# Two chained transformer stacks in one kernel: the residual scaled and rounded piece by piece from its PSUM bank, with some turns, loads and waits moved

## What is computed

```python
def rms_norm(x, g):
    y = x * lax.rsqrt(jnp.mean(x * x, axis=-1, keepdims=True) + RMS_EPS)
    return y * g
def swiglu(x, w13, w2):
    gate, up = jnp.split(x @ w13, 2, axis=-1)
    return (jax.nn.silu(gate) * up) @ w2
# for each layer i of each block, with its gains g[0..7]:
h = h + 0.5 * rms_norm(swiglu(rms_norm(h, g[0]), ffn_w13[i, 0], ffn_w2[i, 0]), g[1])
h = h + rms_norm(mixer(rms_norm(h, g[2])), g[3])
h = h + 0.5 * rms_norm(swiglu(rms_norm(h, g[4]), ffn_w13[i, 1], ffn_w2[i, 1]), g[5])
gate = jax.nn.sigmoid(rms_norm(h, g[6]) @ ple_w_gate[i])
h = h + rms_norm(gate * (p[i] @ ple_w_proj[i]), g[7])
```

## Time and profile before

| | us |
|---|---|
| median of three executions | 2274.13 |
| the profiled execution, its own time | 2272.61 |
| its span, first to last instruction | 2270.8 |
| TensorE busy | 2236.9 (99%) |
| VectorE busy | 1467.1 (65%) |
| ScalarE busy | 1154.9 (51%) |
| GpSimd busy | 180.8 (8%) |

### The profile page before, as it was taken

How to read it: one execution, slowest core, us unless ns; L and a number is a source line. 1 busy time by engine, 2 the same in 40 slices (tenths; PEclk the granted TensorE clock), 3 DMA queues, 4 the chain that set the end, 5 groups by cost and what they waited for, 6 DMA issues and landing times.

```text
span 2270.8 us, 33812 instructions
## 1 busy us (share of the span) xinstructions
PE 2236.9 (99%) x13395; PEld 1820.5 (80%) x13395; DVE 1467.1 (65%) x2079; ACT 1154.9 (51%) x1668; POOL 180.8 (8%) x286
## 2 busy tenths in 40 slices
PE   8999999999999999999999999999999999999998
PEld 6888888888888758878887888878888788868887
DVE  6656757656765877576567656656656765677655
ACT  5445545445544454254455445455445544565444
POOL 1001001001000010420011001001001100051001
PEclk9999999999999999999999999999999999999999
DMA  7556655554655640065556555524555555526553
GB/s 260 183 190 204 230 171 192 186 184 167 213 185 187 203 158 12 8 221 184 185 175 200 185 186 194 189 96 156 184 188 190 187 185 185 194 78 199 185 177 111
DMA packets 290091, 395.61 MB, mean 174 GB/s; under 512 B 11752, under 2 KB 193328, under 8 KB 289936
## 3 DMA queue, kind: packets, MB, share of 16 engines
q1 hardware_dynamic: 285072, 377.20, 50.3%
q0 software_dynamic: 4720, 16.20, 2.1%
q10 hardware_dynamic: 144, 0.07, 0.0%
HBM read 392.37 MB, written 1.05 MB: 173 GB/s over the span
## 4 chain that ended last, share of the span: by engine, by line
PE 94%; DVE 3%; ACT 1%; issue 1%; POOL 0%; DMA 0%; DVEq 0%; POOLq 0%; SPq 0%; ACTq 0%
PE bank L516 28%; PE bank L518 27%; PE bank L517 27%; PE bank L542 2%; PE bank L530 1%; PE bank L2560 0%; PE bank L2554 0%; ACT wh L637 0%; PE bank L1451 0%; ACT JUNK L644 0%; PE bank L2571 0%; PE bank L1966 0%; PE bank L1188 0%; DVE H L890 0%; PE bank L2531 0%
## 5 line engine op out<-in xcount | busy, mean ns | idle before, releaser
L823 DVE TENSOR_TENSOR wl<-raw,wh 128x1024 fp32r<-128x1024 f32 x708 | 859.0, 1223 | 554.8 <-ACT wh L637 554.4
L637 ACT ACTIVATE wh<-raw 128x1024 fp32r<-128x1024 f32 x708 | 744.2, 1058 | 648.1 <-PE bank L518 622.5
L516 PE MATMUL bank<-wh,XH 128*128 128x512 f32 x2000 | 801.0, 400 | 5.2 <-DVE wl L823 2.9
L518 PE MATMUL bank<-wh,XL 128*128 128x512 f32 x2000 | 780.7, 390 | 0.0
L517 PE MATMUL bank<-wl,XH 128*128 128x512 f32 x2000 | 780.5, 390 | 0.0
L516 PEld LDWEIGHTS bank<-wh,XH 128*128 128x128 f32 x2000 | 375.9, 188 | 94.5 <-issue 17.1
L518 PEld LDWEIGHTS bank<-wh,XL 128*128 128x128 f32 x2000 | 375.9, 188 | 81.6
L517 PEld LDWEIGHTS bank<-wl,XH 128*128 128x128 f32 x2000 | 376.5, 188 | 72.1 <-issue 0.5
L516 PE MATMUL bank<-wh,AH 128*128 128x512 f32 x704 | 276.0, 392 | 0.0
L518 PE MATMUL bank<-wh,AL 128*128 128x512 f32 x704 | 274.2, 389 | 0.0
L517 PE MATMUL bank<-wl,AH 128*128 128x512 f32 x704 | 274.1, 389 | 0.0
(11 more groups left out here) (339 smaller groups left out, 1725.3 us busy)
## 6 DMA issues: line engine op xcount, KB each, us to landing
raw<-in_ffn_w_dram SPq DMA_DIRECT2D x182, 512.0 KB, 4.7
raw<-in_ffn_wi_dram SPq DMA_DIRECT2D x176, 512.0 KB, 4.7
raw<-in_ffn_w_dram SPq DMA_DIRECT2D x40, 1024.0 KB, 4.9
raw<-in_ffn_wo_dram SPq DMA_DIRECT2D x40, 1024.0 KB, 4.8
raw<-in_a_wqkv_dram SPq DMA_DIRECT2D x18, 1024.0 KB, 4.8
raw<-in_a_w_in_dram SPq DMA_DIRECT2D x16, 1024.0 KB, 5.2
raw<-in_b_w_in_dram SPq DMA_DIRECT2D x12, 1024.0 KB, 4.9
bc<-in_norm_g_dram POOLq DMA_DIRECT2D x16, 512.0 KB, 5.2
```

Source lines behind the costliest of these rows:

```text
L516: pe.e.matmul(o, a, h, start=(k == 0), stop=False)
L518: m = pe.e.matmul(o, b, h, start=False, stop=(k == layer.nk - 1))
L637: act.e.activation(self.wh[j % N_W][:, 0:p.size], self.raw[p.chunk % N_RAW][:, p.at:p.at + p.size], ACT.Copy).then_inc(*self.rounded.up(j))
L823: dve.e.tensor_tensor(self.wl[j % N_W][:, 0:p.size], self.raw[p.chunk % N_RAW][:, p.at:p.at + p.size], self.wh[j % N_W][:, 0:p.size].bitca ...
```

## The change

- CT and the counter x_scaled are gone. ScalarE now writes XH in four instructions of 128 x 128 for each half, straight from the bank, with the gain as scale. VectorE writes XL in four `scalar_tensor_tensor` of 128 x 128: bank by gain, minus XH. They begin when all four of the half's XH are there. TensorE waits for single squares instead of halves. The bank is free after the last XL of its half.
- Tile 1's turns: steps 8 and 9 in a stage that follows ple or dilated, steps 6 and 7 in all others, stage 0 included.
- Stage 0: tile 1 of x is loaded behind chunk 1; its scaling stands ahead of part 4 instead of part 2; the six `pe_keep` matmuls at step 4 are gone.
- `dve_out`: at the last part of the first half, the result is weighed before that part's `leave`.
- RWKV: LoRA steps 18, 22, 26, 30; ScalarE's `act_mixed(2, 1, 1)` behind th; `pe_keep` in (0, 1) and (1, 1) instead of (0, 1) and (1, 0).

```diff
     def x_ready(self, n):
-        return lambda k, t: [(self.x_hi, n, t, k // 4), (self.x_lo, n, t, k // 4)]
+        return lambda k, t: [(self.x_hi, n, t, k), (self.x_lo, n, t, k)]
     def pe_turn_own(self, pe, n, step):
-        first = 6 if n else 2
+        first = 6 if n == 0 else 8 if STAGES[n - 1][0] in ("ple", "dilated") else 6
     def pe_turn_x(self, pe, n, t, b):
-        bank = self.turn_bank(pe, ("x", n, t, b), (self.x_scaled, n, t, b))
+        bank = self.turn_bank(pe, ("x", n, t, b), (self.x_lo, n, t, 4 * b + 3))
...
         def up(step):
-            if n == 0 and step == 4:
-                pe.wait_all(self.bank_busy[1])
-                self.pe_keep(pe, self.bank(1), 6)
...
+    def x_parts(self, n, t, k):
+        block, c = self.gains(n)
+        turned = self.bank(self.place["turn", ("x", n, t, k // 4)])[:, (k % 4) * P:(k % 4 + 1) * P]
+        to = [x[:, k, t * P:(t + 1) * P] for x in (self.XH, self.XL)]
+        if STAGES[n][0] == "dilated":
+            turned = turned.rearrange("p (b c) -> p c b", c=4)
+            to = [x.rearrange("p (c b) -> p c b", c=4) for x in to]
+        return turned, self.GT[:, block, c + k:c + k + 1], *to
     def act_x_hi(self, act, n, t, b):
-        act.wait_ge(self.x_scaled, n, t, b)
-        act.e.activation(self.XH[:, 4 * b:4 * b + 4, t * P:(t + 1) * P], self.CT[b][:, :, :], ACT.Copy).then_inc(
-            *self.x_hi.up(n, t, b))
+        act.wait_ge(self.consts, "gains" if self.gains(n)[0] == 0 else "gains2")
+        act.wait_ge(self.turned, "x", n, t, b)
+        for k in range(4 * b, 4 * b + 4):
+            turned, gain, hi, _ = self.x_parts(n, t, k)
+            act.e.activation(hi, turned, ACT.Copy, scale=gain).then_inc(*self.x_hi.up(n, t, k))
...
-    def dve_x_lo(self, dve, n, t, b):
-        hi, lo = (x[:, 4 * b:4 * b + 4, t * P:(t + 1) * P] for x in (self.XH, self.XL))
-        dve.wait_ge(self.x_hi, n, t, b)
-        dve.e.tensor_tensor(lo, self.CT[b][:, :, :], hi.bitcast(F32), ALU.subtract).then_inc(*self.x_lo.up(n, t, b))
+    def dve_x_lo(self, dve, n, t, b):
+        dve.wait_ge(self.consts, "gains" if self.gains(n)[0] == 0 else "gains2")
         dve.wait_ge(self.turned, "x", n, t, b)
+        dve.wait_ge(self.x_hi, n, t, 4 * b + 3)
+        for k in range(4 * b, 4 * b + 4):
+            turned, gain, hi, lo = self.x_parts(n, t, k)
+            dve.e.scalar_tensor_tensor(lo, turned, gain, hi.bitcast(F32), ALU.mult, ALU.subtract).then_inc(
+                *self.x_lo.up(n, t, k))
     def dve_x(self, dve, n, t):
-        for b in range(2):
-            self.dve_x_scale(dve, n, t, b)
         for b in range(2):
             self.dve_x_lo(dve, n, t, b)
...
             if i == half - 1:
-                self.leave(dve, p.j + N_W)
                 for t in range(T):
                     self.dve_weigh(dve, n, 0, t, self.pair((n, "out", 0))[t])
+                self.leave(dve, p.j + N_W)
...
             self.load(sp, c)
-            if c == 0:
+            if c == 1:
                 tokens(1)
...
-        if step in (17, 21, 25, 29):
-            b, t = divmod((step - 17) // 4, 2)
+        if step in (18, 22, 26, 30):
+            b, t = divmod((step - 18) // 4, 2)
...
-            self.act_mixed(act, 2, *divmod(i, 2))
+            if i < 3:
+                self.act_mixed(act, 2, *divmod(i, 2))
         if i == 3:
...
+            self.act_mixed(act, 2, 1, 1)
...
-        if (t, o) in ((0, 1), (1, 0)):
+        if o == 1:
             self.pe_keep(pe, banks[0], 6 - t)
```

More of the change, by code:

```diff
@@ L311, in __init__ @@
         self.AL = at("AL", EO + FF // P * S * 4, [P, FF // P, S], F32R)
-        self.CT = [at(f"CT{i}", EO + 54784 + 2048 * i, [P, 4, P], F32) for i in range(2)]
         self.gU = at("gU", EO + 32768, [P, T, 2048], F32)
@@ L417, in __init__ @@
         self.used = [count(f"used{t}") for t in range(T)]
-        self.turned, self.x_scaled, self.x_hi, self.x_lo = (
-            count(x) for x in ("turned", "x_scaled", "x_hi", "x_lo"))
+        self.turned, self.x_hi, self.x_lo = (count(x) for x in ("turned", "x_hi", "x_lo"))
         self.squared, self.rs = count("squared"), count("rs")
@@ L722, in act_start @@
                 self.act_x_hi(act, 0, 0, j)
-            if j == 2:
+            if j == 4:
                 for b in range(2):
@@ L824, in leave @@
                             self.wh[j % N_W][:, 0:p.size].bitcast(F32), ALU.subtract).then_inc(*self.left.up(j))
[L826 to L830, removed]
-        dve.wait_ge(self.turned, "x", n, t, b)
[L832 to L841, removed]
-    def dve_x_lo(self, dve, n, t, b):
-        hi, lo = (x[:, 4 * b:4 * b + 4, t * P:(t + 1) * P] for x in (self.XH, self.XL))
-        dve.wait_ge(self.x_hi, n, t, b)
-        dve.e.tensor_tensor(lo, self.CT[b][:, :, :], hi.bitcast(F32), ALU.subtract).then_inc(*self.x_lo.up(n, t, b))
+    def dve_x_lo(self, dve, n, t, b):
+        dve.wait_ge(self.consts, "gains" if self.gains(n)[0] == 0 else "gains2")
+        dve.wait_ge(self.turned, "x", n, t, b)
+        dve.wait_ge(self.x_hi, n, t, 4 * b + 3)
[3 more added lines that the diff above has]
+                *self.x_lo.up(n, t, k))
     def dve_x(self, dve, n, t):
-        for b in range(2):
-            self.dve_x_scale(dve, n, t, b)
         for b in range(2):
@@ L926, in dve_start @@
         dve.e.memset(self.NEG[:, :], -0.5).then_inc(*self.neg.up())
-        for b in range(2):
-            self.dve_x_scale(dve, 0, 0, b)
         self.dve_x_lo(dve, 0, 0, 0)
@@ L932, in dve_start @@
         self.leave(dve, 1)
-        self.dve_x(dve, 0, 1)
         for j in range(2, N_W):
+            if j == 4:
+                self.dve_x(dve, 0, 1)
             self.leave(dve, j)
```

## The result

Eleven executions of the changed kernel have a median of 2281.54 us (2278.71 to 2291.44), eleven of the kernel before 2274.13 us. The ratio is 1.0031 with a 95% interval of 1.0020 to 1.0041: slower by 0.3%. The profiled execution took 2278.71 us, its span is 2276.9: 6.1 us more than the one before.

What follows compares the result with a forecast made beforehand. TensorE, busy 99% of the span, was taken to bound the kernel. Terms 3.45 + 2.9 - 1.4 - 0.75 - 1.1 - 1.2 - 0.2 gave +1.7: 2274.3 us profiled, 2275.8 median; range 2270.0 to 2282.0.

Steps and rivals of the forecast that it cites:

- the entries to ple: Four boundaries into ple stages: lose nothing, as part 3 is there three steps into the second layer.
- the clock: Rival: TensorE's clock falls in the new stalls; one fall gives 2277.5, two 2279.2, four 2282.6 us; chance 0.33.
- The pieces: Four 128 x 128 instructions per half: ScalarE's end after 1.15 us, VectorE's after 1.14; next may start at 1.06.
- Cheaper: Rival: ScalarE's and VectorE's four hold no more than one copy and one subtraction, 2270.1 or 2267 us; chance 0.17.
- Dearer: Rival: strided dilated reads or VectorE's bank reads cost 0.1 us more a piece, +5 to +8; chance 0.15.
- ple to ffn: Stages 4, 8, 12: VectorE's chain 0.75 us late plus 0.4 for the later turn, together +3.45 us.
- The small boundaries: Stages 1, 2, 9, 13, 14: 0.55 us lost in four places, up to 0.75 at stage 1, together +2.9.
- dilated: Dilated to ffn: with the turn at step 8 the residual is there, -1.4 us.
- rwkv: Rwkv to ffn: weighing in VectorE's idle time makes the residual 1.1 us earlier; -0.75 us net.
- LoRA: RWKV's LoRA step: th no longer behind act_mixed and the product a step later, -1.1 us.
- scan: RWKV scan: extra matmuls of (1, 0) cover nothing and go, those in (1, 1) fit an idle; -1.2 us.
- The start: Stage 0: step 9 at 20.1 against 20.36 us, -0.2, after an idle of 2.2.

Runs made afterwards that it cites:

- the pieces undone: The changed kernel with scale, rounding and rest of x done by whole halves through CT again: 2272.02 us, ratio 0.9986 to the kernel before.
- the turn put back: The changed kernel with tile 1's turns back at steps 6 and 7 behind ple stages: 2281.41 us, ratio 1.0025 to the kernel before.
- the pieces alone: The kernel before with only the four-instruction x_hi and x_lo straight from the bank added: 2284.64 us, ratio 1.0044 to the kernel before.

## Why the prediction came out right

2281.54 lies in the range, 2270 to 2282, but only half a microsecond below its upper end, and outside the forecast's own range, 2273.5 to 2278. The wide range held because it was drawn around the rivals too; that the time fell just inside it is partly luck. Slower by over 0.2% had a chance of 0.32, same 0.58, and it came out slower by 0.3%. The forecast was +1.7 us, the medians are 7.4 apart. From 2275.8 to 2281.5 it is two steps: 1.2 us at the entries to ple, and the clock. The other terms missed by at most 0.3 each, and these misses cancel.

**The pieces** were sized right: four hold ScalarE for 1.02 and end after 1.14 (1.06 and 1.15 forecast), VectorE's four take 1.13 (1.14). An instruction on a bank with a scale and one on tiles in SBUF were good rows for the new ones. ("Those rows read SBUF" is wrong for rows 3: their source is a bank.) "Cheaper" fell: four pieces hold ScalarE for 1.02 and VectorE for 1.04, not for 0.53 and 0.61. The Trainium skill (VectorE: DVE Perf Modes, The TRN2 errata) has the cycles from which the prediction estimated 0.25 us for a piece. A single piece is 375 ns long by the groups, but in a row of four they follow each other after 0.26, so the estimate fits the spacing and not the length. It never led to a chain on time and a sum of -3.7, as the prediction has it: four times 0.25 hold ScalarE for 1.0, nearly the forecast's own 1.06. "Dearer" fell too: the dilated boundary gave 1.55. The Trainium skill (PSUM — Partial Sum Buffer, PSUM bank collisions raise a hardware error) has two engines in one bank as an error even where both read; that fits x_lo waiting for the fourth XH of its half, which was not varied here.

**ple to ffn** held to 0.1 a place. Its two terms stand apart in the runs: 0.7 goes with the pieces undone (0.75 forecast), 0.5 with the turn put back (0.4). That part 3 ends the stall is shown by moving it: the stall at step 7 goes, and 1.75 of its 2.7 comes off the time.

**The small boundaries** were sized 0.3 too high in sum, most of it at stage 1, which lost 0.45 where the prediction took no slack and 0.75.

**The entries to ple** are the step that failed: "lose nothing, part 3 is there three steps into the second layer, and that cover is over 2 us". That is right for the weight part; the turn at step 6 was not priced. Before, it had 0.5 us of slack behind the residual, and the chain was 0.8 late:

```profile
536.98 1.41 DVE L890 SCALAR_TENSOR_TENSOR H<-TMP,ST,H 128x512 f32<-128x512 f32 x2
...
538.34 0.60 PE L530 MATMUL bank<-ident,H 128*128 128x128 f32 x4
```

```profile
540.33 1.41 DVE L881 SCALAR_TENSOR_TENSOR H<-TMP,ST,H 128x512 f32<-128x512 f32 x2
541.23 0.63 PE L527 MATMUL bank<-ident,H 128*128 128x128 f32 x4 [0.15 <-DVE H L881]
```

The idle reads 0.15, the loss is 0.3 (541.23 less 538.34 is 2.89, where the steps before were 2.56 late): TensorE's rows are 0.39 long but 0.23 apart, so a wait is read from start to start.

**The gains** (dilated, rwkv, LoRA, scan) held within 0.15 each. The run with these alone has all four, and loses 0.9 elsewhere.

**The start** was right for step 9 (20.41, forecast 20.1, idle 2.29 for 2.2) and so for its own term; the fall behind it was the rival's.

**The clock.** The rival priced a fall at 1.7, two at 2279.2 for the median and four at 2282.6; the profiled execution has two, 3.3 us of its 6.1, and the median lies between. Filling the stalls without shortening them gives 4.8 us back. It had a chance of 0.33 against 0.35 for the forecast. The sign for it was right, that the clock had fallen 2.0 us after the last matmul and the stalls forecast were longer; the step that was weighed wrongly is "it was a single event with nothing after it". But it was a thin sign: 2.0 is the shortest of the thirteen traces, in which that delay runs up to 5.3 us, and four of fifteen such stalls passed without a fall. The Trainium skill (TensorE: Matmul & The Clock Gate, Why this matters for your kernels) names a longer gap; by that rule the clock would have held, and here it fell behind idles of 2.3 to 2.8 us.

## What to carry to other kernels

An engine that gains in busy time can still lose: VectorE does 10 us less work after the change, but the longer pieces stand ahead of another tile's chain, and each of twelve boundaries passes that on. When a chain becomes later, price every consumer behind it (the turn as well as the weight part), and look for an idle gap ahead of the long group: one `leave` moved there brought the median back to that of the kernel before (2273.38 against 2273.84). A stall on TensorE as long as these is to be priced with a likely fall of the clock (1.65 here, in 11 of 15 places), and where it can't be removed, cheap matmuls that fit within it give that back.

## What the runs showed of the hardware

- At idles of 2.3 to 2.8 us the clock fell in 11 of 15 places of the profiled executions: at the start in six of six, at step 7 behind ple in five of nine. The fall came from 0.55 us before the end of the idle to 1.4 behind it. Each time the clock was low for 3.4 us, which cost 1.65, and down to 1.43 where part of it lay inside the idle. At the ten idles of 1.53 to 1.84 it never fell, and none between 1.84 and 2.29 was seen.
- It also fell in the scan, where TensorE runs small matmuls and no single idle is over 1.0 us: for 17.1 us from 881.3 in one trace, which cost 7.9, and for 6.8 us from 953.7 in another, which cost 3.0. What brings it down there in some executions is open. A time 6 to 9 us above the median at a mean clock of 0.995 or 0.996 came in 16 of 78 executions of the kernel before as well, so it isn't the change's. The one trace of an execution at 0.995, of the pieces alone, has the loss in the scan; that the others have it there is not shown.
- A wait on TensorE that is already met costs nothing that the ledger shows: per-square waits in 15 stages left no entry of their own.
- Four `scalar_tensor_tensor` of 128 x 128 take 1.13 us with a bank as one source, where four on SBUF alone took 1.14.
